# Five taps instead of seven on TensorE, and the sample rows' tap products on GpSimd, in a depthwise convolution loop

## The reference, cut to what matters

```python
a = x @ w_pw1 + b_pw1
u = a[..., :D_MODEL] * jax.nn.sigmoid(a[..., D_MODEL:])
full = jnp.concatenate([hist.astype(u.dtype), u], axis=1)
c = lax.conv_general_dilated(full, w_dw[:, None, :], window_strides=(1,), padding='VALID',
                             dimension_numbers=('NWC', 'WIO', 'NWC'),
                             feature_group_count=D_MODEL) + b_dw
c = jax.nn.silu(layernorm(c, ln_g, ln_b))
y = c @ w_pw2 + b_pw2
```

## Time and profile before

| | us |
|---|---|
| median of 3 runs (lowest to highest) | 1449.43 (1446.32 to 1454.56) |
| the profiled execution | 1449.8 |
| its span, first to last instruction | 1448.0 |

### The profile page before, as it was taken

The page is one execution under the profiler, slowest core; times in us unless marked ns, Lnnn a source line. Parts: engine busy times, 40 slices in busy tenths (PEclk is TensorE's granted clock), DMA queues, the critical chain, the costliest instruction groups (busy, mean ns, idle before and its releaser), DMA issues. The chain is left out here.

```text
span 1448.0 us, 15649 instructions
## 1 busy us (share of the span) xinstructions
PE 1169.1 (81%) x5862; PEld 680.1 (47%) x5862; DVE 530.4 (37%) x959; ACT 265.0 (18%) x482; POOL 123.7 (9%) x204
## 2 busy tenths in 40 slices
PE   6999998939978775299999566499999489788780
PEld 5777653523333332288888543245545334333320
DVE  2799973143322211400000433247721423222215
ACT  3111025210000000300000322146622100000001
POOL 2200010001111110000000100012300011111100
PEclk9999998969988998599999888779999789999995
DMA  8314007077999993232222677650052669999935
GB/s 220 67 34 170 1 4 309 33 282 318 419 420 421 422 399 137 87 94 71 70 68 81 225 290 263 217 168 0 1 217 114 263 267 419 420 421 421 418 131 205
DMA packets 110330, 310.77 MB, mean 215 GB/s; under 512 B 22290, under 2 KB 65042, under 8 KB 85672
## 3 DMA queue, kind: packets, MB, share of 16 engines
q1 hardware_dynamic: 99750, 287.41, 52.2%
q0 software_dynamic: 9216, 17.85, 3.3%
q10 hardware_dynamic: 1298, 4.62, 0.8%
HBM read 295.56 MB, written 29.02 MB: 224 GB/s over the span
## 5 line engine op out<-in xcount | busy, mean ns | idle before, releaser
L1753 PE MATMUL psum<-arena 128*64 128x512 f32 x1024 | 229.3, 600 | 2.8 <-DVE arena L2009 2.8
L1767 PE MATMUL psum<-arena 128*64 128x512 f32 x512 | 143.7, 713 | 65.1 <-DMA arena<-moe_w_down 61.2
L505 PE MATMUL psum<-arena 128*128 128x272 f32 x768 | 179.3, 397 | 6.4 <-DMA arena<-sb_w_qkv 6.4
L505 PEld LDWEIGHTS psum<-arena 128*128 128x128 f32 x768 | 148.0, 193 | 37.6 <-issue 6.8
L1753 PEld LDWEIGHTS psum<-arena 128*64 128x64 f32 x1024 | 81.3, 139 | 144.9 <-issue 141.4
L1331 PE MATMUL psum<-arena 128*128 128x272 f32 x512 | 121.0, 398 | 2.5 <-DVE arena L1541 2.0
L1593 DVE SCALAR_TENSOR_TENSOR arena<-arena,vec 128x512 f32<-128x512 f32 x169 | 114.3, 753 | 0.0
L1767 PEld LDWEIGHTS psum<-arena 128*64 128x64 f32 x512 | 44.8, 161 | 138.7 <-issue 133.2
L1331 PEld LDWEIGHTS psum<-arena 128*128 128x128 f32 x512 | 97.9, 192 | 24.4 <-issue 3.9
L2038 DVE TENSOR_TENSOR arena<-arena,psum 128x256 f32<-128x256 f32 x32 | 13.5, 422 | 216.5 <-ACT arena L1938 216.5
L528 DVE TENSOR_SCALAR arena<-psum 128x272 f32 x24 | 10.6, 442 | 175.4 <-PE psum L505 175.4
(11 more groups left out here) (261 smaller groups left out, 1286.2 us busy)
## 6 DMA issues: line engine op xcount, KB each, us to landing
arena<-moe_w_gate SPq DMA_DIRECT2D x64, 1024.0 KB, 22.6
arena<-moe_w_up SPq DMA_DIRECT2D x64, 1024.0 KB, 28.1
arena<-moe_w_down SPq DMA_DIRECT2D x64, 1024.0 KB, 27.0
arena<-cache_k SPq DMA_DIRECT2D x32, 512.0 KB, 4.5
arena<-cache_v SPq DMA_DIRECT2D x32, 512.0 KB, 4.8
arena<-sb_w_qkv SPq DMA_DIRECT2D x24, 512.0 KB, 3.5
arena<-conv_w_pw SPq DMA_DIRECT2D x16, 512.0 KB, 5.8
arena<-rows_out SPq DMA_DIRECT2D x16, 512.0 KB, 6.5
```

Source lines behind the costliest of these rows:

```text
L505: last = nc.tensor.matmul(K.ps[2 * u + n][:, 0:HALF], wt[u][:, k, :], HT[:, k, n * HALF:(n + 1) * HALF], start=(k == 0), stop=(k == KT - 1))
L1753: last = mm(out[half[q], :].rearrange("t (m f) -> t m f", m=2), xe[:, k, half[q]], w[:, :, k, :], start=(k == 0), stop=(k == KT - 1))
L1767: last = mm(K.ps[4 + n][half[q], :], hT[:, j, half[q]], w[:, j, n * 512:(n + 1) * 512], start=(j == 0), stop=(j == NJ - 1))
```

## The change

Tiles 0 to 6 keep five taps on PE instead of seven; tile 7 keeps 14. The two taps more a tile fall to DVE's list, since it takes what PE leaves. The multiplication of the sample rows' windows goes from DVE's program to POOL's, with the same operands. On POOL it waits for the history copies (before the first), for the tile's gating, and, from the second on, for DVE's reduction of the product before, since there is one buffer `sprod`. The copies of fresh rows follow after the last product. DVE's reduction waits for `sprod`, as before.

```diff
-TAPS_PE, TAPS_LAST = 7, 14
+TAPS_PE, TAPS_LAST = 5, 14
...
             last.then_inc(s["wr"], 1)
-            pool.wait_ge(s["glu"], KT)
+            pool.wait_ge(s["histout"], KT // 2)
+            for ct in range(KT):
+                base = U[:, ct, SAMPLE0:STREAM]
+                win = bass.AP(base.tensor, base.offset, [base.ap[0], [HIST + DS, DB], [1, DS], [1, W]])
+                pool.wait_ge(s["glu"], ct + 1)
+                if ct:
+                    pool.wait_ge(s["sred"], ct)
+                nc.gpsimd.tensor_tensor(sprod, win, vec[:, ct, V_DW:V_DW + W].unsqueeze(1).unsqueeze(1).to_broadcast([P, DB, DS, W]), ALU.mult).then_inc(s["sprod"], 1)
             for k in range(KT):
...
-            def sample_products(ct):
-
-                base = U[:, ct, SAMPLE0:STREAM]
-                win = bass.AP(base.tensor, base.offset, [base.ap[0], [HIST + DS, DB], [1, DS], [1, W]])
-                if ct:
-                    dve.wait_ge(s["sred"], ct)
-                v.tensor_tensor(sprod, win, vec[:, ct, V_DW:V_DW + W].unsqueeze(1).unsqueeze(1).to_broadcast([P, DB, DS, W]), ALU.mult).then_inc(s["sprod"], 1)
-
...
                 done += len(mine)
-                if ct == 0:
-                    dve.wait_ge(s["histout"], KT // 2)
-                sample_products(ct)
                 dve.wait_ge(s["tap"], done)
```

## The result

The changed kernel takes 1458.53 us (median of 19 runs, 1452.59 to 1466.72), the kernel before 1449.56 (19 runs, 1442.62 to 1454.56). The ratio is 1.0066, 95% interval 1.0050 to 1.0081: slower, by some 9 us. The profiled execution took 1458.84, its span 1457.0, 9.0 more than before.

A forecast was written before the change was run, and what follows sets the result against it. DVE bounds early tiles, PE tiles 4 to 6; after the change DVE bounds every tile. Loop +11.5 us and tail -3.6 give +7.9 on the 1449.43 median: 1457.3 us, range 1446 to 1464.

The forecast's parts named there:

- t(0): Start of DVE's gating that opens channel tile 0 in the convolution stage; the prediction's per-tile times count from such gatings.
- The loss a tile: In tiles 0 to 6, GpSimd's product stops DVE's taps: 1.9 us a tile, kept between 1.49 and 2.28.
- DVE's own work: In each loop tile, two more taps add 1.32 us, the product's departure saves 0.98: net +0.35, 20.52 before the stop.
- the give-back: Without the product to cover its wait, DVE's sum of the halves starts 0.12 us later than one tap pitch.
- The loop: Tiles 0 to 6 at a new period of 22.42 us, moving the last tile's gating by +11.5 us.
- t(7): Start of DVE's gating that opens channel tile 7, the last; predicted to move by +11.5 us, to near 204.
- The tail: After the last gating, PE's 14 taps start 5.2 us sooner; with a slowed start the gain is 3.6 us.
- the slowed start of the last taps: In tile 7, PE's idle gap lowers its clock, so the last taps lose 1.66 us.
- the count: Slowed and quick PE tiles alternate from the first long gap, ahead of projection 2, ending with slow last taps.
- One to one to the end: After the last statistics, whatever the loop gains or loses carries unchanged to the kernel's end.
- A: Rival, DVE's taps: GpSimd's product only uses gaps, no loss; loop gains 1.8 us, tail 5.2, giving 1442.4; chance 0.13.
- B: Rival, GpSimd's product: overlapping rows of 31 make it 3.1 us, costing DVE about 2.9 a tile: 1464.3; chance 0.13.

## Why the prediction was right

It forecast 1457.3 us, +7.9; measured were 1458.53 and, in the profile, +9.0. The gatings at t(0), before and after, and PE's granted clock in the first projection, before and after, with the columns of the earlier trace rows:

```profile
44.28 0.50 DVE L1539 SCALAR_TENSOR_TENSOR arena<-psum,vec,arena 128x272 f32<-128x272 f32 x1 [15.09 <-PE psum L1331]
...
45.02 0.50 DVE L1546 SCALAR_TENSOR_TENSOR arena<-psum,vec,arena 128x272 f32<-128x272 f32 x1 [16.78 <-PE psum L1338]
```

```profile
30.00:31.00 1.00, 1.00 (x6) 1.00 1.20 285
...
30.00:31.00 1.00, 1.00 (x4) 0.50 1.38 339
```

Step by step:

- **The loss a tile**, 1.9 us, was the step on which all hung, taken between 1.49 and 2.28. Measured: 2.44 - 0.55 = 1.89 on the first tap, 9.91 - 8.03 = 1.88 in tile 0. The 0.48 of the earlier trace rows had shown it at a third of the size. That the two engines exclude each other was read from the trace; that 1.9, the middle of two bounds, met the size to 0.01 us was luck. The price came from STTs, too, and no row shown then told that it holds for the tensor_scalar that paid (the last section has rows of the kernel before that could have).
- **DVE's own work**: the sum of the halves starts 8.06 after the first of the last twelve taps (105.09 to 113.15), 0.12 beyond twelve pitches of 0.662: the give-back as predicted. Period 22.42, measured 22.41.
- **The loop**: from t(0) = 45.02 to t(7) = 204.80 it takes 159.78 us, against 44.28 to 192.59, 148.31, before. That is +11.5, as predicted.
- **The tail**: the last statistics come 20.29 after t(7), against 23.92: -3.6, as predicted, with the slowed start of the last taps (13.95 - 12.29 = 1.66). Long and short gaps alternated, and the count ended on a long one. That this cost the 1.66 us is in part luck, since a long gap does not always slow what follows: in the run with a second product beside the reduction the same taps came after 3.42 us of idle time and took 12.26, at a granted clock of 1.00 from the start, and with the product in the middle the projection of tile 2 came after 3.08 and took 14.91. With sixteen pieces and with the product in the middle the last taps ran undisturbed, and the whole 5.3 us came back. The merge ended at 17.1 after t(7), predicted 17.2, and held nothing up; the fresh copies were done at 8.0.
- **One to one to the end**: from the last statistics to the end of the span 1231.9 us, before 1231.5. It holds to 0.4.
- **Missed**: t(0) itself came 0.74 later. The first projection took 16.6 instead of 14.9 us, after the same idle time ahead of it; of the kernels profiled here some show the one and some the other, without a pattern that I can tie to their edits, and the loop has not begun by then. The granted clock tells the two apart: from 30 to 31 us it is 0.50, the lower level, in the changed kernel and 1.00 in the kernel before, and in the experiments it is about 0.5 where that projection took 16.6 and 1.00 where it took 14.9. Why it was low is open. With the 0.74, 11.5 - 3.6 + 0.7 + 0.4 = 9.0 accounts for the span's difference.

Of the rivals, A (POOL yields) is out as a matter of this change, but half right as a mechanism: short pieces nearly yield (0.04 us for 62 elements), a long one doesn't. B (the window's shape is dear on POOL) is out: the product took 2.11 us for 992 elements, in proportion even less than the flat addition's 2.35 for 1024.

The Trainium skill's rule that I weighed ("SBUF — State Buffer", section "Who interferes with whom") held in kind, and the runs here show its other side as well: it says that tensor_reduce doesn't contend on this chip and that an instruction with one SBUF input outside the quick modes doesn't, and the reduction kept its 1.18 us and the merge its 0.68 beside the product. Taken literally, with the whole 2.28 us, it came out 0.4 us a tile too dear, and 0.2 with the 2.12 us that the product took.

## What to carry to other kernels

Work that looks free because its engine is idle can be paid for on another engine: look for any place in the trace where the two already overlap, and price the loss from instructions that grow longer there, by the size of the operation. Whether the victim matters depends on who bounds the loop after the change: here the same stop was covered while PE had seven taps, and exposed with five. Then look for instructions of the victim that aren't stopped, and put the work beside those; that turned 1.0066 into 0.9967.

## What the runs showed of the hardware that was not expected

The instruction that paid was not the one of the earlier trace rows. Of the taps it was a tensor_scalar with one SBUF tensor as input that was stopped, 2.44 us instead of 0.55, just as an STT with two is in tile 0; one of 32 elements waited until POOL was done (1.12 instead of 0.24). A reduction over 992 elements with one input is not touched. So the count of inputs alone doesn't tell which instructions are stopped.

Rows of the kernel before, from layer 1, show the same with other instructions: DVE's copies (L802) and a tensor_scalar (L1012) beside selects on POOL (masks that are set by position):

```profile
815.84 2.75 DVE L802 COPY arena<-arena 64x32 f32<-64x32 f32 x4
...
867.80 0.53 DVE L802 COPY arena<-arena 64x32 f32<-64x32 f32 x4
...
984.59 1.01 DVE L1012 TENSOR_SCALAR arena<-psum,sbb 128x768 f32<-128x768 f32 x1
```

```profile
815.19 1.62 POOL L653 TENSOR_SCALAR_AFFINE_SELECT arena<-arena 32x512 f32<-32x512 f32 x1
816.87 1.67 POOL L656 TENSOR_SCALAR_AFFINE_SELECT arena<-arena 32x512 f32<-32x512 f32 x1
...
984.74 0.29 POOL L1034 TENSOR_SCALAR_AFFINE_SELECT arena<-arena 128x128 f32<-128x128 f32 x1 [1.01 <-DVE arena L1027]
```

Four copies with one SBUF input each take 2.75 us beside the two selects and 0.53 without, while the tensor_scalar, which reads PSUM, takes 1.01 us beside a select and 1.02 without one (at 991.43). In these traces, then, DVE was held up in instructions that read SBUF alone, the reduction excepted, and not where a tensor came from PSUM. The selects work on a mask and the copies on other tensors, so a stop does not need a tensor that both engines read, as the product and the stopped taps both read the weights in `vec`.

The stop is by instruction, and of each access of POOL's only a little is hidden, some 0.07 us by the pieces: 0.04 us lost for 62 elements, 0.18 for 124, 0.48 for 320, 1.9 for 992. Cutting the product in sixteen took two thirds of the loss away, but stretched the product to 10 us a tile, as each piece has to wait for one of DVE's instructions to end.
